# Four groups of seven block products in the second down projection, with the weight sums made in HBM

## Chip, cores and metric

One core of a Trainium2 chip runs the whole program, once per launch, in float32. The metric is the device time of one execution in microseconds (us).

## What is computed

Two transformer blocks over 256 tokens of width 1024. The first holds two mixers (forgetting attention and a gated delta rule) and a gated feed-forward part; the second holds neighbourhood attention, a pooling mixer and a gated feed-forward part of hidden width 2816. The change sits in the last product of the second block:

```python
h2 = rms_norm(x, norm2_g[l])
x = x + (jax.nn.silu(h2 @ w_gate[l]) * (h2 @ w_up[l])) @ w_down[l]
```

`w_down` is 2816 x 1024, so this last product takes 256 x 2816 by 2816 x 1024.

## The kernel before

TensorE multiplies float32 as sums of two parts: each weight panel is copied to `panel_hi` by ScalarE (ACT), VectorE (DVE) makes the residual `panel_lo`, and each 128-row tile of a product takes three matmuls (hi by hi, lo by hi, hi by lo). All weight products of both blocks stand in one list, `HALVES`, of 258 **steps**. A plain step uses half a panel: 12 matmuls of 512 columns in the last product. Four buffers each of `panel_hi` and `panel_lo` go round (`whi`, `wlo`): the copy of step n waits until the product of step n - 4 is done (`s_half`). The panels come by SP's DMA queue into three 1 MB buffers `panel_raw`, refilled when the residual of their last step is made (`s_lo`); at the start three more, `panel_raw_early`, are filled ahead. Every engine walks the same list in program order, so an instruction that waits holds all that stands behind it on its engine.

The last product uses seven products in place of eight on part of its rows (Winograd's form of Strassen's scheme). A **group** is 512 rows of `w_down`. Split in even and odd 128-row tiles and in two halves of 512 columns, it gives the blocks b11, b12, b21, b22 (512 KB each); the 256 tokens are two halves. Then

- t1 = b11 + b12, t3 = b12 + b22, t2 = t1 + b22, t4 = t2 + b21 are sums of weight blocks (signs lie in the activations),
- GpSimd (POOL) makes four sums of activations for each pair of row tiles (`act2_sums`), split in hi and lo by ACT and DVE,
- seven **block steps** (b11, b21, b22, t3, t1, t2, t4) of 6 matmuls each go into seven PSUM banks, and DVE combines the banks at the end (`block_sums`).

`GROUP_ORDER` says in which order block steps stand, and where plain steps (`None`) stand between them. Before there are two groups, with every block step but one followed by a plain step; the other 1792 of the 2816 rows are plain. The four blocks of a group are loaded during the product before (`up2`), and the sums are made by DVE in place (`add_block`), each right behind the residual of a block.

Ahead of all this stands the first block's input projection. Its first panels and the small tensors load from the start of the span. POOL's work in that part: one power at the start, one for the key norms (step 17), a mask for each attention head (`mask_key_bias`, which waits for a load of that head), and gate arithmetic.

Of the kernel before, what the change touches and what calls it, by code (L numbers as in the profile page):

```python
# [23 lines left out]
P = 128  # L24
# [46 lines left out]
for _name, _n in (("ident", P), ("upper", P), ("ones", 4), ("causal", P), ("decay_mask", P),  # L71
# [142 lines left out]
TAIL_AT = {n: j for n, (s, j) in TAP_AT.items() if s == 1}  # L214
BLOCKS_FROM = [END["up2", 1, 4], END["up2", 1, 6]]
UP2_AT = {}
# [21 lines left out]

def build(nc, a, out, scratch_a, scratch_x, scratch_c):
    ctx = ExitStack()  # L240
    with ctx:
# [5 lines left out]
        def at(name, shape, unit, dt=F32, skip=0):  # L247
            return nc.alloc_sbuf_tensor_at(name, shape, dt, offset=BASE + int(unit * UNIT) + skip)[:]
# [61 lines left out]
        sq2 = at("sq2", [P, TT, 2, PW], 23.5)  # L310
        block_at = [{"b11": 22, "b12": 22.5, "b21": 23, "b22": 23.5}, {"b11": 0, "b12": 0.5, "b21": 16.5, "b22": 21.5}]
        block_raw = [{b: at(f"block_{b}_{i}", [P, HALF * PW], block_at[i][b]) for b in BLOCKS} for i in range(2)]
        act_sums = [at(f"act_sums{i}", [P, 4, P], 21, skip=2048 * i) for i in range(2)]
        act_sums_hi = at("act_sums_hi", [P, 2 * GROUPS, 4, P], 18, F32R)
        act_sums_lo = at("act_sums_lo", [P, 2 * GROUPS, 4, P], 19.5, F32R)
        sum_u, sum_v, minus_w, p5_less_v = [at(f"block_sum{i}", [P, WIDE], 1, skip=2048 * i) for i in range(4)]
        mixh, mixl = at("mix_hi", [P, KD, T], 11, F32R), at("mix_lo", [P, KD, T], 12, F32R)
# [182 lines left out]
        s_g_low, s_g_row, s_half_rsq = sem("ffn2_low_copied"), sem("ffn2_gate_scaled"), sem("half_row_rms")  # L500
        s_block = [[sem(f"block_row{r}_landed{i}") for r in range(2)] for i in range(2)]
        s_block_add = sem("blocks_added")
        s_sums, s_sums_hi, s_sums_lo = sem("act_sums"), sem("act_sums_hi"), sem("act_sums_lo")
# [90 lines left out]
        def block_rows(g, b):  # L594
            r, c = int(b[1]) - 1, int(b[2]) - 1
            w = weights["w_down_2"][g * HALF * P:(g + 1) * HALF * P, wide(c)]
            return w.rearrange("(k r p) c -> r p k c", r=2, p=P)[r]

# [3 lines left out]

        KEPT_IN = {b: b for b in BLOCKS} | {"t1": "b11", "t3": "b12", "t2": "b22", "t4": "b21"}
        OTHER = {"t1": "b12", "t3": "b22", "t2": "b11", "t4": "b22"}
        ADDS = list(ADDED_BEHIND.values())

        def block_landed(g, b):
            return s_block[g][int(b[1]) - 1], 32

        def block_added(g, b):  # L610
            return s_block_add, len(ADDS) * g + ADDS.index(b) + 1

        def block_ready(g, b):
            return block_landed(g, b) if b in BLOCKS else block_added(g, b)

# [618 lines left out]
        def scalar_program(e):  # L1234
# [3 lines left out]
            def split(n):  # L1238
                if n > STEPS:
                    return  # L1240
                i, k0, kt = HALVES[n - 1]
                if i is None:
                    g, b = k0, kt
                    e.wait_ge(*block_ready(g, b))
                    e.wait_ge(s_half, n - 4)
                    copy(whi[(n - 1) % 4], block_raw[g][KEPT_IN[b]]).then_inc(s_hi, 1)
# [483 lines left out]
        def vector_program(e):  # L1730
            def add_block(g, b, n):
                t_ = ADDED_BEHIND[b]
                to = block_raw[g][KEPT_IN[t_]]
                e.wait_ge(*block_landed(g, OTHER[t_]))
                e.wait_ge(s_lo, n)
                if ADDS.index(t_):
                    e.wait_ge(s_block_add, len(ADDS) * g + ADDS.index(t_))
                e.tensor_tensor(to, to, block_raw[g][OTHER[t_]], ALU.add).then_inc(s_block_add, 1)  # L1738
# [750 lines left out]
        def pool_program(e):  # L2489
# [36 lines left out]
            def act2_sums(j):  # L2526
# [14 lines left out]
            for n in range(1, STEPS + 1):  # L2541
                if n == 27:
                    e.wait_ge(s_consts, 16)
                    mask_key_bias(0)
# [44 lines left out]
        def sync_program(e):  # L2589
            def fetch(i):  # L2590
# [8 lines left out]
                for s in range(parts):  # L2599
                    e.dma_start(dst[:, :, s * n:(s + 1) * n], w_rows(weights[w], k0, kt, c0 + s * apart, n)) \  # L2600
                        .then_inc(raw_landed(i)[0], 16)

            x_rows = a["x"][0].rearrange("(t p) d -> p t d", p=P)
            for c in range(2):
# [10 lines left out]
            for n in range(1, STEPS + 1):  # L2615
                for i in range(9, len(PLAN)):
                    if LAST_HALF[BEFORE[i]] + 1 == n + 3:
                        fetch(i)
                for g in range(GROUPS):
                    for at_, b in zip(range(0, 8, 2), ("b11", "b12", "b21", "b22")):  # L2620
                        if n == BLOCKS_FROM[g] + at_:
                            e.wait_ge(*emptied(("out2", 1, 1)))
                            e.dma_start(block_view(block_raw[g][b]), block_rows(g, b)).then_inc(block_landed(g, b)[0], 16)
                if n == 3:
# [139 lines left out]
```

## Time and profile before

| | |
|---|---|
| Median of 3 runs | 802.75 us (802.33 to 803.99) |
| The profiled execution | 802.98 us, span 801.5 us |
| TensorE busy | 795.6 us (99% of the span), 5164 matmuls recorded |
| DVE, ACT, POOL busy | 625.1, 457.2, 90.7 us |
| DMA | 144.09 MB, 180 GB/s over the span |
| Granted TensorE clock | full speed throughout |

A busy share says how long some instruction ran on an engine. Matmuls overlap each other: their durations add up to more than the time they take, so the time of a run of matmuls is read from its start and end.

### The profile page before, as it was taken

Reading aid. Unit: us, or ns where it says so; the run is one execution under the profiler, and the core shown is the slowest. Engines: PE = TensorE matmul, PEld = TensorE weight load, DVE = VectorE, ACT = ScalarE, POOL = GpSimd, SP = SyncE. Lnnn points to the kernel's source line nnn. Section 1 sums busy time; section 2 is a strip of 40 time slices with the busy share of each in tenths; the row PEclk is TensorE's granted clock in tenths of the full one; section 3 lists DMA queues with packets and bytes.
Section 4 is the critical chain, followed back from the end, with each engine's and each line's share of the span. In section 5 each row is a group of like instructions: output and inputs, shape, how many; then the busy total and the mean of one; then the engine's idle time right before and its main releaser. Section 6 shows DMA issues by size and latency. Waiting matters only on the chain. (4 is left out here: it accounts for less than half of the span.)

```text
span 801.5 us, 13178 instructions
## 1 busy us (share of the span) xinstructions
PE 795.6 (99%) x5164; PEld 696.8 (87%) x5164; DVE 625.1 (78%) x1035; ACT 457.2 (57%) x738; POOL 90.7 (11%) x77
## 2 busy tenths in 40 slices
PE   8999999999999999999999999999999999999998
PEld 6888888999898888899999998887778888888886
DVE  6888989785555766679999997486866898787977
ACT  6667677554535544456656563466665566555552
POOL 0001000010011302101101110011100333011100
PEclk9999999999999999999999999999999999999999
DMA  9654564557432555475687656464424666884331
GB/s 317 187 166 157 176 229 145 151 146 228 123 118 88 172 173 199 167 237 180 193 251 244 224 186 209 165 203 160 156 79 147 198 207 214 288 282 161 107 103 54
DMA packets 118125, 144.09 MB, mean 180 GB/s; under 512 B 11552, under 2 KB 86704, under 8 KB 117808
## 3 DMA queue, kind: packets, MB, share of 16 engines
q1 hardware_dynamic: 115616, 141.22, 54.7%
q10 hardware_dynamic: 2448, 2.03, 1.0%
q8 instruction: 41, 0.67, 0.3%
q14 instruction: 20, 0.16, 0.1%
HBM read 141.78 MB, written 1.46 MB: 179 GB/s over the span
## 5 line engine op out<-in xcount | busy, mean ns | idle before, releaser
L1754 DVE TENSOR_TENSOR panel_lo<-panel_raw,panel_hi 128x1024 fp32r<-128x1024 f32 x237 | 300.8, 1272 | 106.8 <-ACT panel_hi L1236 105.1
L652 PE MATMUL bank<-x_halves,panel_hi 128*128 128x256 f32 (+1 forms) x1536 | 367.0, 322 | 0.7 <-DVE x_halves L2222 0.7
L1236 ACT ACTIVATE panel_hi<-panel_raw 128x1024 fp32r<-128x1024 f32 (+1 forms) x239 | 252.2, 1057 | 152.9 <-PE bank L652 150.8
L652 PE MATMUL bank<-x_halves,panel_lo 128*128 128x256 f32 x1024 | 288.3, 282 | 0.0
L652 PEld LDWEIGHTS bank<-x_halves,panel_hi 128*128 128x128 f32 x1536 | 255.8, 190 | 23.3 <-issue 0.9
L652 PEld LDWEIGHTS bank<-x_halves,panel_lo 128*128 128x128 f32 x1024 | 195.0, 190 | 0.2
L652 PE MATMUL bank<-panel_hi,x_halves 128*128 128x512 f32 x384 | 122.1, 399 | 0.0
L652 PEld LDWEIGHTS bank<-panel_hi,x_halves 128*128 128x128 f32 x384 | 70.0, 188 | 14.4 <-DVE panel_lo L1754 0.6
L652 PE MATMUL bank<-panel_lo,x_halves 128*128 128x512 f32 x192 | 75.1, 391 | 0.0
L652 PE MATMUL bank<-panel_hi,act_hi 128*128 128x512 f32 x156 | 60.9, 390 | 0.2 <-DVE panel_lo L1754 0.2
L652 PE MATMUL bank<-panel_hi,act_lo 128*128 128x512 f32 x156 | 60.7, 389 | 0.0
L652 PE MATMUL bank<-panel_lo,act_hi 128*128 128x512 f32 x156 | 60.7, 389 | 0.0
L652 PEld LDWEIGHTS bank<-panel_lo,x_halves 128*128 128x128 f32 x192 | 36.0, 188 | 8.0
L2491 POOL TENSOR_TENSOR stats<-stats 128x2 f32<-128x2 f32 (+1 forms) x9 | 17.1, 1900 | 185.1 <-DVE stats L1768 104.0
L652 PEld LDWEIGHTS bank<-panel_hi,act_hi 128*128 128x128 f32 x156 | 29.3, 188 | 6.6 <-DVE panel_lo L1754 0.6
L652 PEld LDWEIGHTS bank<-panel_lo,act_hi 128*128 128x128 f32 x156 | 29.3, 188 | 6.1
L652 PEld LDWEIGHTS bank<-panel_hi,act_lo 128*128 128x128 f32 x156 | 29.3, 188 | 5.9
L1790 DVE SCALAR_TENSOR_TENSOR conv_acc<-conv_tmp,params,conv_acc 128x255 f32<-128x255 f32 (+2 forms) x72 | 30.5, 484 | 1.4 <-ACT conv_acc L1236 1.4
L2517 POOL TENSOR_TENSOR ff_tanh<-ff_tanh,ff_val 128x512 f32<-128x512 f32 x11 | 17.2, 1564 | 112.4 <-DVE ff_tanh L2115 112.4
L2496 POOL TENSOR_TENSOR key_bias<-key_bias,constants 128x128 f32<-128x128 f32 x16 | 8.9, 577 | 176.6 <-DMA key_bias<-gate_sums 176.6
L2524 POOL TENSOR_TENSOR f_tanh<-f_tanh,ff_val 128x512 f32<-128x512 f32 x11 | 15.2, 1385 | 94.0 <-DVE f_tanh L2191 94.0
L1748 DVE TENSOR_TENSOR panel_lo<-block_b,panel_hi 128x1024 fp32r<-128x1024 f32 x14 | 18.2, 1301 | 5.2 <-ACT panel_hi L1236 4.8
(312 smaller groups left out, 1017.1 us busy)
## 6 DMA issues: line engine op xcount, KB each, us to landing
panel_raw<-in_w_in SPq DMA_DIRECT2D x35, 1024.0 KB, 5.3
panel_raw<-in_w_up SPq DMA_DIRECT2D x30, 1024.0 KB, 5.4
panel_raw<-in_w_down SPq DMA_DIRECT2D x16, 1024.0 KB, 5.0
panel_raw<-in_w_gate SPq DMA_DIRECT2D x10, 1024.0 KB, 5.4
panel_raw<-in_w_out SPq DMA_DIRECT2D x8, 1024.0 KB, 5.0
panel_raw<-in_w_in SPq DMA_DIRECT2D x11, 512.0 KB, 4.7
panel_raw<-in_w_branch_fox SPq DMA_DIRECT2D x4, 1024.0 KB, 5.0
panel_raw<-in_w_branch_gdn SPq DMA_DIRECT2D x4, 1024.0 KB, 5.0
```

The costliest lines, as they stand in the source:

```text
L652: return e.matmul(o, l, r, start=start, stop=stop, skip_group_check=True)
L1236: return e.activation(o, i_, ACT.Copy, scale=scale)
L1748: e.tensor_tensor(wlo[w], block_raw[g][KEPT_IN[b]], whi[w].bitcast(F32), ALU.subtract) \
L1754: e.tensor_tensor(lo, raw_view(i, k0, kt), hi.bitcast(F32), ALU.subtract).then_inc(s_lo, 1)
L1790: e.scalar_tensor_tensor(acc[:, f, back:], tmp[:, f, 0:T - back], gconv(p, f, back), acc[:, f, back:], ALU.mult, ALU.add).then_inc(s_taps, 1)
L2491: return e.tensor_tensor(cols, cols, minus_half.broadcast_to([P, n]), ALU.pow)
L2496: i_ = e.tensor_tensor(key_bias[:, s], key_bias[:, s], C("causal"), ALU.add)
L2517: e.tensor_tensor(th, th, ff_acc[j % 2][1], ALU.mult).then_inc(s_f_mul, 1)
L2524: e.tensor_tensor(th, th, ff_acc[j % 2][1], ALU.mult).then_inc(s_g_mul, 1)
```

## The change

Groups go from two to four (2048 rows), and plain steps from 14 to 6. The weight sums are no longer made by DVE in SBUF: POOL issues 32 transfers from HBM to HBM, 16 copies and 16 that accumulate into their destination, into a new HBM tensor `weight_sums` of 16 blocks of 512 KB. SP then loads the seven blocks of each group (three of `w_down`, four sums) into a ring of ten 512 KB buffers, two sharing a semaphore. The diff (cut):

```diff
-GROUPS = 2
-DOWN2_ORDER = [(8, 0), (8, 1), (12, 0), (12, 1), (16, 0), (20, 0), (16, 1), (20, 1)]
+GROUPS = 4
+DOWN2_ORDER = [(16, 0), (16, 1), (20, 0), (20, 1)]
-GROUP_ORDER = [("b11", None, "b21", None, "b22", None, "t3", None, "t1", None, "t2", None, "t4", None),
-               ("b11", None, "b21", None, "b22", None, "t3", None, "t1", "t2", None, "t4", None, None)]
-ADDED_BEHIND = {"b11": "t1", "b21": "t3", "b22": "t2", "t3": "t4"}
+GROUP_ORDER = [(None, "b11", "b21", "b22", "t3", "t1", "t2", "t4"),
+               (None, "b11", "b21", "b22", "t3", "t1", "t2", "t4"),
+               ("b11", "b21", "b22", "t3", "t1", "t2", "t4"),
+               ("b11", "b21", "b22", "t3", "t1", "t2", "t4", None, None, None, None)]
+WEIGHT_SUMS = ("t1", "t3", "t2", "t4")
+SUM_ROUNDS = (2, 5, 7, 8)
+SUMS_FROM, SUMS_EVERY = 11, 5
+SUMS_AT = {SUMS_FROM + SUMS_EVERY * i: divmod(i, len(SUM_ROUNDS)) for i in range(GROUPS * len(SUM_ROUNDS))}
...
-                    e.tensor_tensor(wlo[w], block_raw[g][KEPT_IN[b]], whi[w].bitcast(F32), ALU.subtract) \
-                        .then_inc(s_lo, 1)
-                    if b in ADDED_BEHIND:
-                        add_block(g, b, n)
+                    e.tensor_tensor(wlo[w], block_buffer(g, b), whi[w].bitcast(F32), ALU.subtract).then_inc(s_lo, 1)
...
+            def copied(g, t_, b):
+                e.dma_start(sum_rows(g, t_), block_rows(g, b)).then_inc(s_weight_sums, 16)
+            def added(g, t_, what):
+                e.dma_start(sum_rows(g, t_), what, accum_op=ALU.add, max_dma_last_dim=4 * WIDE).then_inc(s_weight_sums, 16)
+            def weight_sums(g, stage):
+                done = SUM_ROUNDS[-1] * g + (SUM_ROUNDS[stage - 1] if stage else 0)
+                if done:
+                    e.wait_ge(s_weight_sums, 16 * done)
+                if stage == 0:
+                    copied(g, "t1", "b11")
+                    copied(g, "t3", "b12")
+                if stage == 1:
+                    added(g, "t1", block_rows(g, "b12"))
+                    added(g, "t3", block_rows(g, "b22"))
+                    copied(g, "t2", "b22")
+                if stage == 2:
+                    added(g, "t2", sum_rows(g, "t1"))
+                    copied(g, "t4", "b21")
+                if stage == 3:
+                    added(g, "t4", sum_rows(g, "t2"))
...
+                for q, (g, b) in enumerate(BLOCK_SEQ):
+                    if q < 6 and n == BLOCKS_FROM + 2 * q:
+                        e.wait_ge(*emptied(("out2", 1, 1)))
+                        fetch_block(q, g, b)
+                    if 6 <= q < len(block_raw) and n == END["up2", 1, KF // 2 - 1] + 1:
+                        e.wait_ge(*product(("up2", 1, KF // 2 - 1)))
+                        fetch_block(q, g, b)
+                    if q >= len(block_raw) and n + 3 == BLOCK_AT[BLOCK_SEQ[q - len(block_raw)]]:
+                        e.wait_ge(s_lo, n + 3)
+                        fetch_block(q, g, b)
```

So a group's sums are made in four **stages** (0 to 3), placed at POOL's steps 11, 16, 21 and so on up to 86. Each stage waits for all transfers of the stage before.

POOL's program begins so before (`stats` holds the small vectors of the norms, and the four rows of `key_bias` shown as x12 are masks of attention heads):

```order
L2491 TENSOR_TENSOR stats<-stats 128x2
L2491 TENSOR_TENSOR stats<-stats 128x16
L2496 TENSOR_TENSOR key_bias<-key_bias,constants 128x128 x12
L2503 TENSOR_SCALAR gate_f<-gate_f 128x512 x2
```

and so after, with stages 0 and 1 of the first group ahead of the key norms and all four of the second between the masks of heads 0 and 1:

```order
L2490 TENSOR_TENSOR stats<-stats 128x2
L2537 DMA weight_sums<-in_w_down 256x1x512 x2
L2540 DMA weight_sums<-in_w_down 256x1x512 x2
L2537 DMA weight_sums<-in_w_down 256x1x512
L2490 TENSOR_TENSOR stats<-stats 128x16
L2540 DMA weight_sums<-weight_sums 256x512
L2537 DMA weight_sums<-in_w_down 256x1x512
L2540 DMA weight_sums<-weight_sums 256x512
L2495 TENSOR_TENSOR key_bias<-key_bias,constants 128x128 x2
```

The power at the start is now followed by five transfers that wait for no other engine's work, only for each other.

ACT's copies near the end stood so before, around the copy of one product's bank (`block_sum`), which waits for that product and for a DVE addition:

```order
L1236 ACTIVATE panel_hi_58<-block_b_1_141 128x1024
L1236 ACTIVATE panel_hi_59<-panel_raw_50 128x1024
L1236 ACTIVATE block_sum_147<-bank 128x512
L1236 ACTIVATE panel_hi_56<-block_b_1_142 128x1024
L1236 ACTIVATE panel_hi_57<-panel_raw_50 128x1024
```

and after it stands in the fourth group, between blocks:

```order
L1247 ACTIVATE panel_hi_58<-block_137 128x1024
L1247 ACTIVATE panel_hi_59<-block_138 128x1024
L1247 ACTIVATE panel_hi_56<-block_139 128x1024
L1247 ACTIVATE block_sum_149<-bank 128x512
L1247 ACTIVATE panel_hi_57<-block_140 128x1024
```

The steps on both sides of it are now block steps of 6 matmuls, where plain steps of 12 stood between blocks.

## Rows read from the trace of the kernel before

**Rows 1.** The page's first part: engine, busy us and share, instructions.

```profile
PE 795.6 (99%) x5164; PEld 696.8 (87%) x5164; DVE 625.1 (78%) x1035; ACT 457.2 (57%) x738; POOL 90.7 (11%) x77
```

**Rows 2.** The chain that ended last: start us, us, what.

```profile
754.89 43.83 PE bank L652 x192
...
798.74 0.48 DVE h L2083
```

**Rows 3.** The timeline at the last product's first matmul: start us, us, what.

```profile
740.88 0.39 PE L652 MATMUL bank<-panel_hi,act_hi 128*128 128x512 f32 x1
```

**Rows 4.** Instruction groups by shape, 742 to 801.5 us: count, busy us, mean ns, idle before.

```profile
L1754 DVE TENSOR_TENSOR panel_lo<-panel_raw,panel_hi 128x1024 fp32r<-128x1024 f32 x13 | 15.9, 1222 | 3.0 <-ACT panel_hi L1236 2.7
...
L1236 ACT ACTIVATE panel_hi<-block_b 128x1024 fp32r<-128x1024 f32 x12 | 12.7, 1060 | 5.1 <-PE bank L652 5.1
...
L1738 DVE TENSOR_TENSOR block_b<-block_b,block_b 128x1024 f32<-128x1024 f32 x7 | 8.6, 1226 | 1.0 <-issue 0.5
...
L2050 DVE SCALAR_TENSOR_TENSOR h<-bank,stats,h 128x512 f32<-128x512 f32 x1 | 0.7, 746 | 0.0
```

**Rows 5.** ACT's timeline in the last product: start us, us, what, idle before.

```profile
750.73 0.64 ACT L1236 ACTIVATE act_hi<-f_tanh 128x512 fp32r<-128x512 f32 x1 [3.04 <-POOL f_tanh L2524]
...
773.25 0.60 ACT L1236 ACTIVATE block_sum<-bank 128x512 f32<-128x512 f32 x1 [1.95 <-DVE h L2050]
773.75 1.05 ACT L1236 ACTIVATE panel_hi<-block_b 128x1024 fp32r<-128x1024 f32 x1
```

**Rows 6.** The page's DMA issues: count, KB each, median us to landing.

```profile
panel_raw<-in_w_in SPq DMA_DIRECT2D x35, 1024.0 KB, 5.3
...
block_b<-in_w_down SPq DMA_DIRECT2D x8, 512.0 KB, 7.2
...
panel_raw<-in_w_down SPq DMA_DIRECT2D x4, 512.0 KB, 3.5
```

**Rows 7.** Stretches: us, busy us of PE to POOL, clock, DMA share, GB/s.

```profile
8.00:12.00 4.00, 2.95 (x19) 1.94 (x19) 3.62 (x9) 3.29 (x7) 0.07 (x1) 1.00 1.10 348
16.00:20.00 4.00, 4.00 (x36) 4.00 (x35) 4.00 (x11) 2.99 (x4) 0.00 (x0) 1.00 1.07 363
24.00:28.00 4.00, 4.00 (x24) 3.47 (x23) 3.19 (x6) 3.16 (x6) 0.00 (x0) 1.00 1.07 371
...
32.00:36.00 4.00, 4.00 (x22) 3.35 (x21) 4.00 (x10) 2.62 (x3) 0.00 (x0) 1.00 0.25 71
...
200.00:250.00 50.00, 50.00 (x465) 43.93 (x462) 26.04 (x55) 22.95 (x48) 4.89 (x8) 1.00 0.34 103
```

**Rows 8.** The tile panel_raw_early: its loads (first and last start), and time to landing.

```profile
L2600 SPq DMA_DIRECT2D panel_raw_early<-in_w_in x3: 1420/2025/2832, 5.2 to 10.2; - x3
...
DMA to landing us min/median/max: 10.7/11.3/11.5
```

**Rows 9.** ACT's timeline, copies of the second and third early panel.

```profile
23.69 1.06 ACT L1236 ACTIVATE panel_hi<-panel_raw_early 128x1024 fp32r<-128x1024 f32 x1 [0.60 <-PE bank L652]
...
26.52 1.06 ACT L1236 ACTIVATE panel_hi<-panel_raw_early 128x1024 fp32r<-128x1024 f32 x1 [0.55 <-PE bank L652]
```

**Rows 10.** POOL's timeline: the first power, and masks of heads 0, 1, 4 and 6.

```profile
7.35 0.72 POOL L2491 TENSOR_TENSOR stats<-stats 128x2 f32<-128x2 f32 x1 [6.54 <-DVE stats L1768]
...
108.76 1.06 POOL L2496 TENSOR_TENSOR key_bias<-key_bias,constants 128x128 f32<-128x128 f32 x2 [38.70 <-DMA key_bias<-gate_sums]
171.37 0.89 POOL L2496 TENSOR_TENSOR key_bias<-key_bias,constants 128x128 f32<-128x128 f32 x2 [61.54 <-DMA key_bias<-gate_sums]
...
206.71 0.88 POOL L2496 TENSOR_TENSOR key_bias<-key_bias,constants 128x128 f32<-128x128 f32 x2 [9.56 <-DMA key_bias<-gate_sums]
...
237.07 0.88 POOL L2496 TENSOR_TENSOR key_bias<-key_bias,constants 128x128 f32<-128x128 f32 x2 [12.19 <-DMA key_bias<-gate_sums]
```

**Rows 11.** Waits over the span: us in total, times, longest us.

```profile
DVE fox_p L1998 <- POOL key_bias L2496: 2.8, 3, 1.6
...
ACT panel_hi L1236 <- DMA panel_raw<-in_w_in: 2.0, 3, 0.8
```

More of the change, by code:

```diff
@@ L83 @@
 DOWN_ORDER = [(k, c) for k in range(0, KF - 6, HALF) for c in range(2)] + [(k, c) for c in range(2) for k in (16, 20)]
-GROUPS = 2
-DOWN2_ORDER = [(8, 0), (8, 1), (12, 0), (12, 1), (16, 0), (20, 0), (16, 1), (20, 1)]
+GROUPS = 4
+DOWN2_ORDER = [(16, 0), (16, 1), (20, 0), (20, 1)]
 BLOCKS = ("b11", "b12", "b21", "b22")
-GROUP_ORDER = [("b11", None, "b21", None, "b22", None, "t3", None, "t1", None, "t2", None, "t4", None),
-               ("b11", None, "b21", None, "b22", None, "t3", None, "t1", "t2", None, "t4", None, None)]
-ADDED_BEHIND = {"b11": "t1", "b21": "t3", "b22": "t2", "t3": "t4"}
+GROUP_ORDER = [(None, "b11", "b21", "b22", "t3", "t1", "t2", "t4"),
+               (None, "b11", "b21", "b22", "t3", "t1", "t2", "t4"),
+               ("b11", "b21", "b22", "t3", "t1", "t2", "t4"),
+               ("b11", "b21", "b22", "t3", "t1", "t2", "t4", None, None, None, None)]
+BLOCK_SEQ = [(g, b) for g, order in enumerate(GROUP_ORDER) for b in order if b]
+WEIGHT_SUMS = ("t1", "t3", "t2", "t4")
+SUM_ROUNDS = (2, 5, 7, 8)
+SUMS_FROM, SUMS_EVERY = 11, 5
 BLOCK_BANK = {"b11": ("p1",), "b21": ("down2", 0, 0), "b22": ("down2", 1, 0), "t4": ("down2", 0, 1), "t1": ("p5",),
@@ L214 @@
 TAIL_AT = {n: j for n, (s, j) in TAP_AT.items() if s == 1}
-BLOCKS_FROM = [END["up2", 1, 4], END["up2", 1, 6]]
+BLOCKS_FROM = END["up2", 1, 4]
+SUMS_AT = {SUMS_FROM + SUMS_EVERY * i: divmod(i, len(SUM_ROUNDS)) for i in range(GROUPS * len(SUM_ROUNDS))}
 UP2_AT = {}
@@ L236, with build @@
 GA_EXP, GA_BETA, GA_COEF, GA_KDEC, GA_MINUS_EGC = 1, 2, 3, 4, 6
-def build(nc, a, out, scratch_a, scratch_x, scratch_c):
+def build(nc, a, out, scratch_a, scratch_x, scratch_c, scratch_w):
     ctx = ExitStack()
@@ L310, in build @@
         sq2 = at("sq2", [P, TT, 2, PW], 23.5)
-        block_at = [{"b11": 22, "b12": 22.5, "b21": 23, "b22": 23.5}, {"b11": 0, "b12": 0.5, "b21": 16.5, "b22": 21.5}]
-        block_raw = [{b: at(f"block_{b}_{i}", [P, HALF * PW], block_at[i][b]) for b in BLOCKS} for i in range(2)]
-        act_sums = [at(f"act_sums{i}", [P, 4, P], 21, skip=2048 * i) for i in range(2)]
+        block_at = (22, 22.5, 23, 23.5, 0, 0.5, 1, 1.5, 2, 2.5)
+        block_raw = [at(f"block{i}", [P, HALF * PW], unit) for i, unit in enumerate(block_at)]
+        act_sums = [at(f"act_sums{i}", [P, 4, P], 16.5, skip=2048 * i) for i in range(2)]
         act_sums_hi = at("act_sums_hi", [P, 2 * GROUPS, 4, P], 18, F32R)
-        act_sums_lo = at("act_sums_lo", [P, 2 * GROUPS, 4, P], 19.5, F32R)
-        sum_u, sum_v, minus_w, p5_less_v = [at(f"block_sum{i}", [P, WIDE], 1, skip=2048 * i) for i in range(4)]
+        act_sums_lo = at("act_sums_lo", [P, 2 * GROUPS, 4, P], 20, F32R)
+        sum_u, sum_v, minus_w, p5_less_v = [at(f"block_sum{i}", [P, WIDE], 10, skip=2048 * i) for i in range(4)]
         mixh, mixl = at("mix_hi", [P, KD, T], 11, F32R), at("mix_lo", [P, KD, T], 12, F32R)
@@ L500, in build @@
         s_g_low, s_g_row, s_half_rsq = sem("ffn2_low_copied"), sem("ffn2_gate_scaled"), sem("half_row_rms")
-        s_block = [[sem(f"block_row{r}_landed{i}") for r in range(2)] for i in range(2)]
-        s_block_add = sem("blocks_added")
+        s_block = [sem(f"blocks_landed{i}") for i in range(len(block_at) // 2)]
+        s_weight_sums = sem("weight_sums_written")
         s_sums, s_sums_hi, s_sums_lo = sem("act_sums"), sem("act_sums_hi"), sem("act_sums_lo")
@@ L596, in block_rows, with sum_rows, block_source, block_buffer @@
             w = weights["w_down_2"][g * HALF * P:(g + 1) * HALF * P, wide(c)]
-            return w.rearrange("(k r p) c -> r p k c", r=2, p=P)[r]
+            return w.rearrange("(k r p) c -> r k p c", r=2, p=P)[r]
+        def sum_rows(g, t_):
+            return scratch_w[g, WEIGHT_SUMS.index(t_)].rearrange("(k p) c -> k p c", p=P)
+        def block_source(g, b):
+            return (block_rows(g, b) if b in BLOCKS else sum_rows(g, b)).rearrange("k p c -> p k c")
         def block_view(t_):
             return t_.rearrange("p (k c) -> p k c", c=WIDE)
-        KEPT_IN = {b: b for b in BLOCKS} | {"t1": "b11", "t3": "b12", "t2": "b22", "t4": "b21"}
-        OTHER = {"t1": "b12", "t3": "b22", "t2": "b11", "t4": "b22"}
-        ADDS = list(ADDED_BEHIND.values())
+        def block_buffer(g, b):
+            return block_raw[BLOCK_SEQ.index((g, b)) % len(block_raw)]
+        def block_sem(q):
+            return s_block[q // 2 % len(s_block)]
         def block_landed(g, b):
[L608 to L614, printed above, removed]
+            q = BLOCK_SEQ.index((g, b))
+            return block_sem(q), 16 * sum(block_sem(i) is block_sem(q) for i in range(min(q | 1, len(BLOCK_SEQ) - 1) + 1))
         def rows_of(sums, h0, n):
@@ L1243, in split @@
                     g, b = k0, kt
-                    e.wait_ge(*block_ready(g, b))
+                    e.wait_ge(*block_landed(g, b))
                     e.wait_ge(s_half, n - 4)
-                    copy(whi[(n - 1) % 4], block_raw[g][KEPT_IN[b]]).then_inc(s_hi, 1)
+                    copy(whi[(n - 1) % 4], block_buffer(g, b)).then_inc(s_hi, 1)
                     return
@@ L1730, in vector_program @@
         def vector_program(e):
[L1731 to L1738, printed above, removed]
             def split(n):
@@ L2541, in pool_program @@
             for n in range(1, STEPS + 1):
+                if n in SUMS_AT:
+                    weight_sums(*SUMS_AT[n])
                 if n == 27:
@@ L2601, in fetch, with fetch_block @@
                         .then_inc(raw_landed(i)[0], 16)
+            def fetch_block(q, g, b):
+                if b not in BLOCKS:
+                    e.wait_ge(s_weight_sums, 16 * SUM_ROUNDS[-1] * GROUPS)
+                e.dma_start(block_view(block_raw[q % len(block_raw)]), block_source(g, b)).then_inc(block_sem(q), 16)
             x_rows = a["x"][0].rearrange("(t p) d -> p t d", p=P)
@@ L2618, in sync_program @@
                         fetch(i)
[L2619 to L2623, printed above, removed]
+                for q, (g, b) in enumerate(BLOCK_SEQ):
[8 more added lines that the diff above has]
+                        fetch_block(q, g, b)
                 if n == 3:
@@ L2760 @@
     sc = nc.dram_tensor("gate_sums", (2, HEADS, T), F32).ap()
-    build(nc, args, out, sa, sx, sc)
+    sw = nc.dram_tensor("weight_sums", (GROUPS, len(WEIGHT_SUMS), PW, WIDE), F32).ap()
+    build(nc, args, out, sa, sx, sc, sw)
     r = run_bass_kernel_spmd(nc, [arrays], core_ids=[0])
```

## The prediction

> **What bounds the kernel now.** I read the page's busy shares first: TensorE is busy for 795.6 of 801.5 us [rows 1]. A busy share of matmuls proves little, so I looked for waits. The chain that ended last goes back over 43.83 us of unbroken matmuls, and behind them stand only DVE's last additions [rows 2]. Over the whole span ACT's copies waited for a panel's load 2.0 us in three cases, so loads are hidden almost everywhere [rows 11]. TensorE is the bound from some 10 us to the end. What the change saves on TensorE is saved in full, and every wait that it puts before TensorE costs in full: there is no slack downstream to take it up.
>
> **TensorE's saving.** Before, the last product has 14 plain steps of 12 matmuls and 14 block steps of 6: 252. After, 6 plain and 28 block steps: 240. The unbroken stretch gives 43.83 us for 192 matmuls, 228.3 ns each [rows 2] (the 390 ns or so that one lasts by itself is no price, as they overlap). Twelve fewer: **-2.74 us**. The whole product ran from 740.88 to 798.72 us, 57.84 us [rows 2, 3]; after, that would be 55.1.
>
> **DVE and ACT in the last product.** DVE loses eight additions of 1.23 us, ACT and DVE gain six steps' copies (1.06 us) and residuals (1.22 us) [rows 4]. That is not the point; the pace is. A block step is 6 x 228.3 = 1.37 us of TensorE, and now up to fourteen and more follow each other without a plain step between. The copy of step n starts when product n - 4 is done; copy and residual take 2.28 us, and three block steps give 4.11. So 1.8 us is spare at each step, and DVE's 1.22 us per step fits in 1.37. It holds, but nothing else may stand in the way for long. Two things do:
>
> - Behind the last gate products ACT waits for POOL's product (3.04 us idle before `act_hi` [rows 5]), and the copies of the next blocks stand behind that. Before, this ended in a short wait of TensorE just ahead of 754.89 us (the unbroken stretch starts there). Block steps reach the place sooner, but DVE's additions there are gone; I take it as unchanged, 0.
> - The copy of the first product's bank (`block_sum`). Put 0 where TensorE ends the last b11. DVE is then at the residual of the step three ahead: copy from -1.37 to -0.3, residual to 0.9. Its addition of 0.75 us [rows 4] ends at 1.65; ACT copies the bank, and its next block copy starts 0.50 us later [rows 5], at 2.15 or somewhat over, and ends at 3.2; the residual ends at 4.45. TensorE wants it at 4.11. With signals between engines I take **+0.5 us**; without them it is 0.3, with a second such wait 1.0.
>
> **Loads in the last product.** Six blocks are loaded before it, as eight were. Left are 22 blocks and a panel of 512 KB, 12.0 MB. The highest rates that the trace holds over some microseconds are 348 to 371 GB/s [rows 7]; at 360, 12.0 MB takes 33.4 us, and the last landing is some 3.5 us behind its issue [rows 6]: 37. The last block step ends at 55.1 less four plain steps (11.0) = 44.1, so its copy must start by 40.4. That leaves 3 us. One block takes 1.46 us to load and 1.37 to use, so the ring of ten falls back by 0.09 us a block, 2 us over 22. I take 0. At 300 GB/s the 12.0 MB take 40.0 us and the end comes 3 us late.
>
> **The 32 transfers of the sums.** The trace holds no transfer from HBM to HBM, none that accumulates and none issued by POOL. I bound them by passes of 512 KB at 360 GB/s, 1.46 us each: below, one pass a transfer (47 us of all DMA engines together); above, every read and write counts, two passes for a copy and three for an accumulation (117 us). They are spread over some 310 us, in which the DMA share is at places as low as 0.34 [rows 7]. What counts is where they meet a tight load or hold POOL.
>
> - *The start.* POOL's first power ends at 8.1 us [rows 10], and stage 0 follows at once: into the stretch where the DMA engines are full, until 28 us [rows 7]. Panels in flight are held back by what the sums put between their packets. The first early panel lands at 5.2 + 10.7 = 15.9 us [rows 8]; TensorE ends step 4 at 23.7 [rows 9], so its copy must start by 23.7 - 2.28 = 21.4: 5.5 us spare, against 2.9 to 5.8 us for stage 0 (2 to 4 passes). The third lands at 10.2 + 11.5 = 21.7 at most; step 5 ends at 26.5 [rows 9], three steps of 2.83 later step 9 begins, at 35.0, and the copy must start by 32.7: 11.0 us spare, against stages 0 and 1 together, 7.3 to 17.4 us (5 to 12 passes). So the cost is 0 to 6.4 us. I take **+0.3**: of all rows a plain load, one pass, is nearest to these, and DMA falls to a share of 0.25 by 32 us [rows 7], so what is late then is caught up.
> - *POOL's queue.* A stage waits for the one before it, and masks stand behind it. The second group's four stages lie between the masks of heads 0 and 1, where POOL idled 61.5 us [rows 10]; stages 0 to 2 take at most 17 passes (25 us) and three landings of 7.2 us [rows 6], 46. In the third group stage 1 is issued behind the mask of head 4, at 207.6 us, and stage 2, which waits for it, stands ahead of that of head 6, at 237.07 [rows 10]: 29.5 us, against 8 passes and a landing, 19. DVE waits for these masks as it is, by up to 1.6 us [rows 11], so a late one goes straight to TensorE. I take 0.
> - *Accumulating beside panels elsewhere.* Loads of 1 MB land 5.3 us after issue [rows 6] and were hardly ever waited for. 0, with up to 2 us if two stages meet a tight panel.
>
> **Sum.** 802.98 (the profiled execution; 1.5 us lie outside its span) - 2.74 + 0.5 + 0.3 = 801.0; that execution lies 0.2 above the median of the runs, so **800.8 us**.
>
> **Rivals.**
>
> *A. The early panels are late.* For it: the full DMA engines until 28 us, and that nothing holds stage 0 back. Against it: 5.5 and 11 us of slack. Above 1 of the 6.4 us, the time is 801.8 to 807. It decides from the point where stages 0 and 1 cost the third early panel over 11 us, so some 7 to 8 passes.
>
> *B. The transfers run on few of the DMA engines.* A copy's source is 2 rows of tiles x 128 x 512, its destination 256 x 512. If the split over engines goes by the outer size 2, two engines carry 256 KB each. A full engine moves 360 / 16 = 22.5 GB/s, so that is 11.7 us for one pass, 35 for three. Then panels that share those two engines wait for them. Stage 0 on the first early panel: 6.4 us of its bytes remain at 9.5 us, and as many of the copy go between them, 6.4 us at one pass and 12.8 at two, against 5.5: 0.9 to 7.3 us late. And stage 1 with three passes takes 35 + 7.2 = 42 us against 29.5 at head 6: its mask is 12.7 us late. Light form: about 802. Heavy form: 7.3 + 12.7 on top, near 820. Nothing in the trace speaks for or against it, since all DMAs there have 128, 64, 16 or 8 rows outermost.
>
> The Trainium skill has a rule of just this form ("DMA: Bandwidth & Descriptors", section "Why a DMA increments its semaphore by 16 and not by 1"): the engine count is the largest one up to 16 that divides the slowest size of both patterns, which would be 2 here, with an exception for some direct copies of GpSimd that get all 16. No run here shows it. By that rule the time is that of rival B, by its exception that of the sum.
>
> *C. The blocks come late in the last product.* 28 block steps want 0.524 MB in 1.37 us, 383 GB/s, above anything that the trace shows for long. For it: the eight block loads before landed in 7.2 us, though issued behind a panel. Against it: ten buffers. At 300 GB/s: 803.8; at 270 (12.0 MB in 44.4 us), 808. It decides below some 330 GB/s.
>
> *D. The product runs without any wait*, those of before gone with DVE's additions: 802.75 - 2.74 - 0.4 = 799.6.
>
> **How the numbers follow.** A difference under 0.2% (1.6 us: under 801.15 is faster, over 804.35 slower) can hardly be told from none here. The forecast has 0.50, and lies near that line: 0.36 of it faster, 0.14 not told from before. A 0.16 (0.07 same, 0.09 slower). B 0.18 (light 0.08 same, heavy 0.10 slower). C 0.10 (0.01 same, 0.09 slower). D 0.06, faster. So faster 0.42, same 0.30, slower 0.28. The range 799.0 to 810 leaves out the heavy half of B and the far end of the gains; the forecast's own is 799.8 to 802.
>
> **What would show it.** Right: some 240 matmuls in about 55.5 us from the first one on `act_hi` to the end; a wait of TensorE of 0.5 us behind the last b11; ACT's copies in the last product released by products, not by DMA. In the first 40 us TensorE as busy as before, the early panels landing 3 to 7 us later. POOL's masks at the same distance from their loads. Wrong: ACT's waits for `panel_raw` or blocks far over 2 us in total; masks that wait for `weight_sums`; a DMA share in the last product at its ceiling with ACT waiting for blocks. Most likely to break the forecast are the prices of the accumulations, of which no row tells.

## The result and the profile after

The changed kernel takes 930.9 us (median of 6 runs, 927.47 to 938.86) against 802.44 us: a ratio of 1.1604, 95% interval 1.1576 to 1.1633. The forecast was 800.8 us, the range to 810. So the loss is 128 us, and it lies ahead of the last product, as the stretches of the profile after show (the stretch, then its length and the busy us and count of PE, PEld, DVE, ACT and POOL; then granted clock, DMA share, GB/s):

```profile
150.00:200.00 50.00, 35.88 (x255) 34.69 (x254) 23.71 (x56) 15.90 (x21) 4.91 (x3) 0.86 0.52 131
200.00:250.00 50.00, 25.73 (x336) 25.11 (x337) 14.33 (x31) 10.26 (x20) 7.76 (x9) 0.73 0.56 134
...
396.00:405.00 9.00, 0.00 (x0) 0.00 (x0) 0.00 (x0) 0.00 (x0) 0.00 (x0) 0.50 0.14 33
400.00:450.00 50.00, 12.35 (x50) 10.47 (x51) 6.25 (x7) 5.29 (x6) 7.51 (x6) 0.58 0.35 86
```

TensorE, busy without a gap from 200 to 250 us before [rows 7], is busy for half of that stretch and for a quarter of 400 to 450. From 396 to 405 us no engine computes at all. Where TensorE stands still the granted clock falls to 0.50, the lower level (1.2 GHz); so its busy time over the span rises to 810.0 us, with 12 matmuls fewer.

Whom does it wait for? TensorE's waits after (us in total, times, longest):

```profile
PE bank L801 <- POOL gate_g L2587: 48.5, 2, 45.6
PE bank L663 <- DVE stats L1997: 47.9, 4, 26.5
PE bank L663 <- DVE panel_lo L1753: 9.5, 3, 6.7
...
DVE fox_p L1997 <- POOL key_bias L2495: 65.1, 5, 29.6
```

`gate_g` is written by POOL's gate sums, and L1997 is the line of DVE that waits for POOL's masks (the last row: 65.1 us in five cases; 2.8 us before [rows 11]). Four fifths of TensorE's waits of 118 us go back to POOL, and POOL's own timeline says what it does (start, us, what, and idle time before with its releaser):

```profile
8.05 1.32 POOL L2537 DMA_DIRECT2D weight_sums<-in_w_down  x1
...
31.37 3.85 POOL L2540 DMA_DIRECT2D weight_sums<-in_w_down  x2 [20.90 <-DMA weight_sums<-in_w_down]
...
222.37 1.17 POOL L2495 TENSOR_TENSOR key_bias<-key_bias,constants 128x128 f32<-128x128 f32 x2
...
261.36 1.90 POOL L2540 DMA_DIRECT2D weight_sums<-in_w_down  x1
292.47 1.90 POOL L2540 DMA_DIRECT2D weight_sums<-in_w_down  x1 [29.20 <-issue]
293.55 1.93 POOL L2537 DMA_DIRECT2D weight_sums<-in_w_down  x1
294.65 1.71 POOL L2495 TENSOR_TENSOR key_bias<-key_bias,constants 128x128 f32<-128x128 f32 x2
...
451.51 2.78 POOL L2587 TENSOR_TENSOR gate_g<-gate_g,gate_f 128x512 f32<-128x512 f32 x2
```

Two things hold it. Between stages it waits for its own transfers: 164.9 us in eleven cases, such as the 20.90 us before 31.37. And five times it stands idle ahead of a *further* transfer of the same stage, named "issue" because no semaphore explains it (29.20 us ahead of 292.47, while the addition issued at 261.36 is under way): 115.8 us. In the waits after (us in total, times, longest; one more, of 1.7 us, is for another kind of transfer):

```profile
POOL weight_sums L2540 <- DMA weight_sums<-in_w_down: 163.2, 10, 24.9
...
POOL weight_sums L2540 <- issue: 62.7, 2, 33.5
...
POOL weight_sums L2537 <- issue: 53.1, 3, 30.9
```

The mask of head 1, at 171.37 us before [rows 10], comes at 222.37; the last gate sum, in POOL's timeline before at

```profile
319.68 3.54 POOL L2563 TENSOR_TENSOR gate_g<-gate_g,gate_f 128x512 f32<-128x512 f32 x2 [8.27 <-DVE gate_g L2022]
```

comes at 451.51, 131.8 us later, right behind the last transfer, and TensorE waits 45.6 us for a gate sum. That is the whole loss to within half a microsecond: the span grew by 129.4 us, and the last product won 2.0.

Why do the transfers take so long? The page's issues (count, KB, median us to landing):

```profile
panel_raw<-in_w_in SPq DMA_DIRECT2D x35, 1024.0 KB, 11.4
...
weight_sums<-in_w_down POOLq DMA_DIRECT2D x24, 512.0 KB, 17.0
...
weight_sums<-weight_sums POOLq DMA_DIRECT2D x8, 512.0 KB, 6.9
...
panel_raw_early<-in_w_in SPq DMA_DIRECT2D x3, 1024.0 KB, 21.0
```

A transfer between two contiguous places (an addition too) lands in 6.9 us, one from `w_down` in 17.0 at the median and an addition from there in up to 35.3. In 396 to 405 us above one addition is alone with the end of a panel's load, and the DMA share is 0.14, at 33 GB/s: two of sixteen engines are 0.125. The queues in that stretch (q0 is POOL's, q1 SP's):

```profile
q0 software_dynamic: 73, 0.15, 8.9%
q1 hardware_dynamic: 72, 0.14, 4.8%
```

The two queues moved almost equal numbers of packets, 73 and 72, with little more than two engines busy: as it seems, the panel's last packets take turns with the addition's on the same two engines. A panel of `w_in` now lands in 11.4 us, 5.3 before [rows 6], and the early ones in 21.0, 11.3 before [rows 8]. Per transfer the engine time is small: in 264 to 290 us q0 shows 13.8% of 16 engines, 57 engine-microseconds for an addition. Over two engines that is 29 us at most, over sixteen 3.6 (estimates).

The last product went as worked out: from its first matmul at 872.31 to the end of the last at 928.12, 55.8 us (forecast 55.6; 57.84 before [rows 2, 3]). The wait of 0.5 us behind the last b11 is there too (the first row is the first matmul; then the chain of the profile after, TensorE idle from 912.33):

```profile
872.31 0.39 PE L663 MATMUL bank<-panel_hi,act_hi 128*128 128x512 f32 x1
...
883.47 23.43 PE bank L663 x102
...
909.22 0.76 DVE h L2049
...
910.00 0.02 ACT block_sum L1247
...
912.86 15.27 PE bank L663 x66
```

### The profile page after: what moved, and what is told of

It reads as the page before. It is cut to its first block, busy times and chain, and to the rows that moved or that the text cites. A ratio compares the mean times of both kernels' runs of the same rounds, so it can differ in the third digit from the quotient of the medians.

```text
span 930.9 us, 13244 instructions
## 1 busy us (share of the span) xinstructions
PE 810.0 (87%) x5152; PEld 707.9 (76%) x5152; DVE 628.7 (68%) x1037; ACT 464.6 (50%) x748; POOL 141.9 (15%) x121
## 4 chain that ended last, share of the span: by engine, by line
PE 53%; DMA 23%; issue 14%; DVE 5%; POOL 3%; ACT 1%; SPq 1%; ACTq 0%; DVEq 0%; POOLq 0%
PE bank L663 51%; DMA weight_sums<-in_w_down 15%; DMA panel_raw<-in_w_in 3%; DMA panel_raw_early<-in_w_in 2%; DVE panel_lo L1753 2%; DVE conv_acc L1789 1%; POOL weight_sums L2540 1%; DMA key_bias<-gate_sums 1%; DMA weight_sums<-weight_sums 1%; DVE panel_lo L1750 1%; ACT panel_hi L1247 1%; POOL gate_g L2587 1%; PE bank L779 1%; DMA gate_sums<-minus_c_rows 1%; PE bank L1101 0%
## 5 line engine op out<-in xcount | busy, mean ns | idle before, releaser
L663 PE MATMUL bank<-x_halves,panel_hi 128*128 128x256 f32 (+1 forms) x1536 | 374.2, 326 | 13.7 <-DVE panel_lo L1753 9.5
L1753 DVE TENSOR_TENSOR panel_lo<-panel_raw,panel_hi 128x1024 fp32r<-128x1024 f32 x229 | 291.8, 1277 | 104.6 <-ACT panel_hi L1247 102.0
L1247 ACT ACTIVATE panel_hi<-panel_raw 128x1024 fp32r<-128x1024 f32 (+1 forms) x231 | 243.5, 1055 | 171.8 <-PE bank L663 138.4
L663 PEld LDWEIGHTS bank<-x_halves,panel_hi 128*128 128x128 f32 x1536 | 262.0, 195 | 37.5 <-DVE panel_lo L1753 10.5
L663 PE MATMUL bank<-panel_hi,act_hi 128*128 128x512 f32 x136 | 53.1, 391 | 0.1
L663 PE MATMUL bank<-panel_lo,act_hi 128*128 128x512 f32 x136 | 52.9, 389 | 0.0
L663 PE MATMUL bank<-panel_hi,act_lo 128*128 128x512 f32 x136 | 52.9, 389 | 0.0
L663 PE MATMUL bank<-fox_pT,vf 128*128 128x128 f32 x48 | 9.5, 348 | 47.9 <-DVE stats L1997 47.9
L1997 DVE CUSTOM_DVE_ANT_0 fox_p<-bank,key_bias 128x128 f32<-128x128 f32 (+1 forms) x16 | 5.1, 354 | 67.3 <-POOL key_bias L2495 65.1
L663 PEld LDWEIGHTS bank<-fox_pT,vf 128*128 128x128 f32 x48 | 7.9, 241 | 49.1 <-DVE stats L1997 48.9
L1750 DVE TENSOR_TENSOR panel_lo<-block,panel_hi 128x1024 fp32r<-128x1024 f32 x28 | 34.9, 1261 | 7.1 <-ACT panel_hi L1247 5.2
## 6 DMA issues: line engine op xcount, KB each, us to landing
panel_raw<-in_w_in SPq DMA_DIRECT2D x35, 1024.0 KB, 11.4
```

What stands on the lines that cost most here:

```text
L663: return e.matmul(o, l, r, start=start, stop=stop, skip_group_check=True)
L1247: return e.activation(o, i_, ACT.Copy, scale=scale)
L1750: e.tensor_tensor(wlo[w], block_buffer(g, b), whi[w].bitcast(F32), ALU.subtract).then_inc(s_lo, 1)
L1753: e.tensor_tensor(lo, raw_view(i, k0, kt), hi.bitcast(F32), ALU.subtract).then_inc(s_lo, 1)
L1997: i_ = e.tensor_tensor_reduce(pb[:, s], bank[:, s], key_bias[:, s], -1.0, -3 * NEG, ALU.add, ALU.min, nm[:, m:m + 1])
```

## Experiments

**Sixteen engines, and no transfers at all.** First theory (E): the outer sizes, 256 and 2, put a transfer on two engines. `spread` turns both sides so that 128 rows stand outermost:

```diff
-                e.dma_start(sum_rows(g, t_), block_rows(g, b)).then_inc(s_weight_sums, 16)
+                e.dma_start(sum_rows(g, t_).rearrange("k p c -> p k c"), block_rows(g, b).rearrange("k p c -> p k c")).then_inc(s_weight_sums, 16)
```

and the same in `added`.

> Both sides of all 32 transfers are written with 128 rows outermost (128 x 2 x 512 instead of 256 or 2 x 128 outermost); same bytes, same places, same waits. Theory E (few engines: the outer sizes 256 and 2 put a transfer on two DMA engines): a transfer from w_down takes about a sixteenth of its 30 or 60 engine-microseconds, 2 to 4 us, plus a few us of landing, so copies land in 4 to 7 us instead of 17 and additions in 6 to 9 instead of 30; masks and gate sums are back at their old times; 800 to 806 us. Rival H (it is the reading and writing of HBM within an accumulation that is slow, on however many engines): additions from w_down stay above 20 us, the time above 860 us. Rival Q (POOL's own issuing is slow): issue lengths and idle times named issue stay, the time above 880 us.

Measured: 806.77 us, ratio 1.0052 (1.0035 to 1.0069). Of 128 us, 124 are gone by the order of sizes alone. Its issues:

```profile
weight_sums<-in_w_down POOLq DMA_DIRECT2D x24, 512.0 KB, 7.2
...
panel_raw_early<-in_w_in SPq DMA_DIRECT2D x3, 1024.0 KB, 13.8
```

No idle time named issue is left, and DVE waits for masks 2.4 us in all. E holds, H and Q fall. The turned form also leaves fewer packets, so one may ask whether it is their number that cost. First the change, then `spread` (packets and sizes of all queues; POOL's packets, MB and share of 16 engines):

```profile
DMA packets 156782, 167.39 MB, mean 180 GB/s; under 512 B 40992, under 2 KB 116144, under 8 KB 156464
...
q0 software_dynamic: 35328, 17.01, 9.5%
...
DMA packets 128110, 167.17 MB, mean 207 GB/s; under 512 B 12320, under 2 KB 87472, under 8 KB 127792
...
q0 software_dynamic: 6656, 16.78, 8.8%
```

The 28,672 packets that are gone are all under 512 B (8 bytes each in the trace). The 6,144 packets that carry POOL's data are the same in both, and by size in the two traces they take 1,154 us of engine time in the change and 1,134 in `spread`. The work is the same; it lies on more engines.

What remains lies 0.8 us above E's range. TensorE waits 4.6 us for DVE's `kT`, and the chain before it starts with the third early panel (start, us, what):

```profile
9.91 21.41 DMA panel_raw_early<-in_w_in
...
41.32 0.61 DVE kT L1803
```

`no_sums` leaves the transfers out and prices the rest of the change:

```diff
-                if n in SUMS_AT:
-                    weight_sums(*SUMS_AT[n])
...
-            return (block_rows(g, b) if b in BLOCKS else sum_rows(g, b)).rearrange("k p c -> p k c")
+            return block_rows(g, {"t1": "b11", "t3": "b12", "t2": "b22", "t4": "b21"}.get(b, b)).rearrange("k p c -> p k c")
...
```

and SP's wait for the sums goes too.

> The 32 transfers are left out, and the 16 blocks of sums are loaded from the places of plain blocks in w_down instead, so the last product computes with unsummed blocks; everything else as in the change. This prices all of the change but the transfers. Theory: only the last product differs from before, 55.8 us against 57.84, so 800.4 us (799.8 to 801.2), a ratio of 0.9975. Rival: some of the 128 us comes from elsewhere in the change (buffers moved, blocks issued between panels), then above 802.5 us.

Measured: 800.22 us, ratio 0.9973 (0.9961 to 0.9985). Without the transfers the change gains 2.3 us, 2.0 of it in the last product; all of the loss belongs to the transfers.

**Four engines.** `four` makes each transfer two of 256 KB with 4 outermost:

```diff
-                e.dma_start(sum_rows(g, t_), block_rows(g, b)).then_inc(s_weight_sums, 16)
+                for k in range(2):
+                    to, what = (t.rearrange("k (p a) c -> k a p c", a=4)[k] for t in (sum_rows(g, t_), block_rows(g, b)))
+                    e.dma_start(to, what).then_inc(s_weight_sums, 16)
```

> Each transfer is two of 256 KB, each with an outer size of 4 on both sides (rows taken in the order 4 x 32). Theory E: four engines for each half, so an addition of 256 KB has half of the 60 engine-microseconds over four engines, 7.5 us, and a copy 3.8 us, plus landing: 9 to 12 and 6 to 8 us; the time is 803 to 825 us, far nearer to spread than to 930.9. Rival H: additions remain near 30 us or above. If the count of engines follows something other than the outer size (128 rows in all, say), it equals spread.

Measured: 815.34 us in one run, idle times named issue 32.4 us, and landings of

```profile
weight_sums<-in_w_down POOLq DMA_DIRECT2D x48, 256.0 KB, 9.4
```

With 2, 4 and 128 outermost the time is 931, 815 and 807 us, so it follows the outer size and not the rows in all. (`four` also halves the transfers, so that a stage has twice as many, which may lie on different engines.) That is the Trainium skill's rule ("DMA: Bandwidth & Descriptors", section "Why a DMA increments its semaphore by 16 and not by 1"): the engine count is the largest number up to 16 that divides the slowest size of both sides. The DMA share of 0.14, the 6.9 us of the contiguous transfers (256 outermost on both sides) and these three times agree with it. So do the packets of 8 bytes. The change has 28,672 of them and `four` 18,432. That is 14 and 12 times the data packets that one of two or of four engines would carry, 2,048 and 1,536, as if each idle engine got a small packet in place of each of these (estimate, from the packet counts); `spread` has none. The rule's exception for some of GpSimd's direct copies did not apply here.

**POOL's queue or the loads?** `dve_masks` leaves the transfers as changed and moves masks, affine maps and gate sums to VectorE:

```diff
-                e.wait_ge(s_kb, hh + 1)
+                e.wait_ge(s_kb_in, 32 * (hh + 1))
+                for s in (slice(0, P), slice(2 * P, 3 * P)):
+                    i_ = e.tensor_tensor(key_bias[:, s], key_bias[:, s], C("causal"), ALU.add)
+                i_.then_inc(s_kb, 1)
+                e.wait_ge(s_kb, hh + 1)
```

and likewise in `branch`, with POOL's calls taken out.

> As changed, two-engine transfers and all, but the causal masks, the affine maps of the gates and the gate sums are done by VectorE instead of POOL, so that nothing that TensorE waits for by way of masks and gate sums stands behind a transfer in POOL's queue. Theory P (the time is lost in POOL's queue): the 96 us of TensorE's waits for masks (47.9) and gate sums (48.5) go, and with them most of the time at the lower clock; 815 to 840 us. Rival L (the loads of panels that share the two engines are what is slow, and the masks only hide it): 870 to 920 us, with the waits now at panel_lo behind panel_raw.

Measured: 891.21 us in one run, in L's range, but not by L's mechanism: `panel_lo` accounts for 12.4 us of TensorE's waits, and the longest is

```profile
PE bank L811 <- POOL stats L2501: 30.2, 1, 30.2
```

the next instruction that stands behind the transfers in POOL's program, the power behind the output projection:

```profile
439.23 0.90 POOL L2551 DMA_DIRECT2D weight_sums<-weight_sums  x1 [14.58 <-DMA weight_sums<-in_w_down]
439.84 1.04 POOL L2501 TENSOR_TENSOR stats<-stats 128x2 f32<-128x2 f32 x1
```

Before it stood at

```profile
349.04 1.62 POOL L2491 TENSOR_TENSOR stats<-stats 128x2 f32<-128x2 f32 x1 [25.82 <-DVE stats L1768]
```

It is 90.8 us late, and the span is 88.4 us longer (90.4 with the 2.0 won at the end). Of its 440 us up to there POOL waits 347 for its own transfers or at their issue, so I read what TensorE loses earlier, to loads, as lying in the shadow of POOL's chain. So I had left out that POOL's queue has a next customer; P's mechanism holds, its price does not.

**Place or form?** `two_89_5` moves the two-engine transfers as they are to a part without masks:

```diff
-SUMS_FROM, SUMS_EVERY = 11, 5
+SUMS_FROM, SUMS_EVERY = 89, 5
```

> The change's own two-engine transfers, at the steps of spread_89_5 (89 to 164). In the change POOL waited 280.7 us for its own transfers or at their issue, and some 30 us went into issuing: 310 us for 16 stages, 19 a stage, where five steps take 14. Theory F (the form of the transfers is what costs, wherever they lie): POOL falls behind by 5 to 7 us a stage, its gate products and powers with it, and TensorE waits for them: 860 to 910 us, with idle times named issue over 60 us. Rival G (the early place, in front of masks and small transfers, is what costs): 801 to 830 us.

Measured: 978.35 us in one run, beyond F's 910. POOL now holds the first feed-forward, and then `norm_gained`, which stands behind the last stage but one (waits in us in total, times, longest; POOL's timeline, before and in `two_89_5`):

```profile
ACT act_hi L1247 <- POOL ff_tanh L2516: 137.5, 10, 37.0
...
DVE norm_junk L1759 <- POOL norm_gained L2508: 53.2, 1, 53.2
...
523.32 2.84 POOL L2509 TENSOR_TENSOR norm_gained<-h,gain_final 128x1024 f32<-128x1024 f32 x1 [43.06 <-DVE h L2032]
...
700.20 1.43 POOL L2537 DMA_DIRECT2D weight_sums<-in_w_down  x1
701.29 2.70 POOL L2508 TENSOR_TENSOR norm_gained<-h,gain_final 128x1024 f32<-128x1024 f32 x1
```

It is 178.0 us late, and the span is 175.5 us longer. The loss is again the lateness of POOL. The panels that land late have moved with the transfers: `w_in` takes 5.3 us again, `w_up` 10.4 instead of 5.4. Form, not place.

**What holds POOL at the issue?** `free_copies` issues 32 two-engine copies, each to a place of its own, without any wait; `free_half` the same with half of the rows. The last product takes unsummed blocks in both.

```diff
-                done = SUM_ROUNDS[-1] * g + (SUM_ROUNDS[stage - 1] if stage else 0)
-                if done:
-                    e.wait_ge(s_weight_sums, 16 * done)
...
+                for slot in range(SUM_ROUNDS[stage - 1] if stage else 0, SUM_ROUNDS[stage]):
+                    copied(g, slot, BLOCKS[slot % 4])
```

> All 32 transfers are plain copies of blocks in the change's own two-engine form, each to a place of its own, so no stage waits for the one before it; the sums are not made and the last product takes unsummed blocks. Nothing in the program holds POOL any more. Theory I (POOL is held at the issue itself, while an earlier transfer is still on its two engines): idle times named issue of 15 us and more ahead of further copies, over 60 us in total, masks late behind them, 820 us or more. Rival S (it was the waits between the stages that held POOL): no such idle times, masks on time, 801 to 808 us, what is left being panels that share engines.

Measured: 829.17 us in one run, idle times named issue 59.3 us in four cases. POOL's timeline, the first of them:

```profile
77.31 2.17 POOL L2538 DMA_DIRECT2D weight_sums<-in_w_down  x2
96.86 1.06 POOL L2538 DMA_DIRECT2D weight_sums<-in_w_down  x1 [17.39 <-issue]
```

The holds come at the 8th, 15th, 22nd and 29th copy. So I is right that POOL is held with no wait in the program. But no mask was late by it (1.8 us of waiting for masks in all). Of the 27 us over the kernel before, TensorE's longest waits show 16.4: 6.6 us for the small transfer of `XT` of the inversion, 5.3 for `panel_lo`, 4.5 for a convolution. I read them as loads that share engines with the copies; the rest is not accounted for.

> As free_copies with the first half of each block's rows alone: 32 two-engine copies of 256 KB, no waits between them. In free_copies POOL was held at the 8th, 15th, 22nd and 29th copy. Theory R (what fills up at the issue is room that goes by the bytes or rows of a transfer): held at about the 15th or 16th and the 29th or 30th alone. Theory N (it goes by the number of transfers): held at the 8th, 15th, 22nd and 29th again. By either the loads are disturbed half as much: 808 to 818 us.

Measured: 805.02 us in one run, a smaller disturbance than either theory said; held twice, at the 16th copy (12.35 us) and the 31st:

```profile
130.07 0.81 POOL L2538 DMA_DIRECT2D weight_sums<-in_w_down  x1 [12.35 <-issue]
...
294.84 0.80 POOL L2538 DMA_DIRECT2D weight_sums<-in_w_down  x1 [12.86 <-issue]
```

So seven copies of 512 KB pass between two holds, and fifteen of 256 KB: theory R. Their queues count 33280 and 16896 packets, 1040 and 528 a copy; 7 x 1040 = 7280 and 15 x 528 = 7920 fit, 8 x 1040 = 8320 and 16 x 528 = 8448 do not. So there is room for about 8,000 packets (estimate, from these counts), and the copy that finds none waits until those under way have ended. It is not the bytes: `spread` moves the same bytes in 6656 packets and was never held. Nor is it only the packets under way: five of the first seven copies in `free_copies` were issued by 14 us and no copy took over 30.0 us to land, so these five had ended long before the hold that began at 79 us. The count seems to go on until it is full and to start afresh there. In the change itself, with additions among the copies, the holds do not fall where this count alone puts them: that is open. They do go by the order of the transfers and not by the time, since they stand at the 7th, 10th, 13th, 20th and 28th transfer in the change, in `dve_masks` and in `two_89_5`.

**The early panels, and a version that gains.** `spread` with the stages elsewhere: steps 18, 23, ... (behind the power of the key norms), 18, 22, ..., then 89, 94, ... and 100, 104, .... The edit is the line of numbers shown for `two_89_5`.

> As spread, with the first stage at step 18 instead of 11, so that POOL comes to it only behind the power of the key norms (66 us) and no transfer meets the early panels; stages 5 steps apart as in the change. Theory A (what spread still lacks of 800.2 is only the early panels that come late, 6.5 us): 800.0 to 801.0 us, a ratio of 0.997 to 0.9985, DVE's wait for kT gone, the early panels landing after 11.3 us again. Rival B2 (the transfers cost about the same wherever they lie, in panels that come late or masks that wait): 803 to 807 us.

> As spread_18_5 with the stages 4 steps apart, so the last lies at step 78 and ahead of the gate sums. Theory A: as spread_18_5 within 0.5 us. Rival B2: 1 to 3 us more than spread_18_5, since the stages lie closer to the masks and a stage that waits for the one before it holds POOL up to 9 us.

Measured: 802.06 and 802.11 us, ratios 0.9995 (0.9985 to 1.0005) and 0.9997 (0.9984 to 1.001). Between A and B2: the early panels land after 11.4 us again and DVE's wait for `kT` is gone, 4.7 us won, but 1.9 us are still missing. Some of it lies from 150 to 200 us. In `spread_18_4` (a profile of a run at the median) TensorE is idle there for 1.3 us, in `spread_18_5` (a profile of a run of 804.76 us, 2.7 above the median) for 1.2 us, for other reasons:

```profile
PE bank L1050 <- DVE fox_p L2008: 1.3, 1, 1.3
...
PE bank L663 <- DMA X<-blocks_inverted: 1.2, 1, 1.2
```

Their runs differ by up to 5 us, so this is no full account.

> As spread, with the stages at steps 89, 94, ... 164, all behind the inversion's small transfers and the masks, over the first feed-forward, in which POOL has only gate products with 10 us between them. Theory A2 (the 1.9 us that spread_18_5 and spread_18_4 lack of 800.2 are meetings with the small transfers and loads of 150 to 200 us): 800.0 to 800.9 us, ratio 0.997 to 0.9985, faster than before. Rival B2 (16 MB more through the DMA engines cost 2 us wherever they lie): 801.5 to 803 us.

> As spread_89_5 at steps 100 to 160, closer together and clear of the power behind the output projection (step 97). Theory A2: within 0.4 us of spread_89_5. Rival B2: 801.5 us or more.

Measured: 800.83 and 800.69 us, ratios 0.9974 (0.9964 to 0.9985) and 0.9975 (0.9964 to 0.9985): A2, and both faster than the kernel before, by a quarter of a per cent. Over the first feed-forward the 16 MB cost at most 0.6 us against `no_sums`; a panel of `w_up` lands in 6.0 us there, and POOL waits up to 10 us for its transfers. ACT waits 7.7 us in all for POOL's products there; TensorE shows one wait of 0.4 us for a residual. The page's busy shares, over a span of 799.8 us:

```profile
PE 792.1 (99%) x5152; PEld 693.8 (87%) x5152; DVE 627.2 (78%) x1037; ACT 463.7 (58%) x748; POOL 140.1 (18%) x121
```

## Why the prediction was wrong, point by point

- **TensorE's saving, DVE and ACT in the last product, loads there:** right. 55.8 us for 55.1 + 0.5, the wait at `block_sum` in its place, the 22 blocks and the panel on time; `no_sums` 800.22 us. Rivals C and D fall.
- **The price of the transfers:** right as a sum, wrong in its shape; this is the first step that failed. In bounds of 47 to 117 us of all DMA engines, the trace has 9.5% of 16 engines over 930.9 us, 88 us. The prediction took passes at 360 GB/s, the rate of all engines, because "of all rows a plain load, one pass, is nearest": but a plain load has 128 rows outermost, and these have 256 against 2. The time to land is what stages and panels wait for: 17.0 us at the median on two engines, 7.2 with 128 outermost.
- **Rival B** named this, with 11.7 us for one pass and 35 for three (measured: copies land in 17.4 us at the median, an addition keeps its two engines for up to 29), and the chance was set to 0.18 because no row spoke for or against it. The sizes stood in the diff, but no row before says what they do. The form was right; its time of 820 was not, for the reason that follows.
- **POOL's queue, "I take 0":** the second failed step, and the larger one. Even rival B counted one late mask, 12.7 us, and ended near 820. Two things were missing. The stages follow each other on POOL, so their lateness adds up over four groups instead of being lost at one mask: what counts is how late the instruction behind the transfers is that others still wait for (131.8 us in the change, 90.8 in `dve_masks`, 178.0 in `two_89_5`, each within 1 us of the loss and the 2 us won at the end). And POOL is also held at the issue, 115.8 us of the change, which no row before shows. No run tells how much of the lateness is these holds and how much the slow landings: `spread` takes both away.
- **The start, +0.3 (rival A at 0.16):** hidden in the change behind the rest, but wrong once the transfers are spread: moving the stages behind the early panels, from `spread` to `spread_18_5`, is worth 4.7 us, inside rival A's 0 to 6.4. The slack was counted to the wrong place. In `spread` the third early panel lands at 31.3 us instead of 21.7 at most, 9.6 us late and within the 11.0 us up to TensorE's own step; but DVE's convolutions stand behind its residual, and TensorE waits for `kT`, which they feed.
- **Loads elsewhere, "hardly ever waited for", 0 to 2 us:** also wrong for two-engine transfers: in the change ACT's copies wait 28.2 us in six cases for panels of `w_in`, 2.0 before [rows 11], and TensorE waits 9.5 us for residuals.

## What to carry to other kernels

Before a transfer is priced, look at the outermost sizes of both its sides as the instruction carries them: merged rows on one side and a size of 2 on the other put it on two engines here, and a turned pattern with the same bytes took 124 of 128 us back. On an engine that issues transfers and waits for them, add up the landings of the whole chain and ask how late the first instruction behind it comes; moving another engine's work out of the way only finds the next one. And a transfer that nobody waits for still has to be put where no load is tight: the same 16 MB cost 6.5, 1.9 and at most 0.6 us at three places.

## What was not expected of the hardware

- POOL stands still when it issues a further transfer, with no semaphore to wait for, after every 7,280 packets of copies in `free_copies` and 7,920 in `free_half`, also where part of them had long landed; the next one had to wait for those under way. In the change such a hold lasted up to 33.5 us.
- The count of packets depends on the form: 1040 for a two-engine copy of 512 KB, of which 896 are of 8 bytes, and 208 on average for the transfers of `spread`, with none of 8 bytes.
- Two transfers of this form in flight at once seem to lie on different pairs of engines: from 412 to 432 us of the change a copy and an addition run together at a DMA share of 0.24, 3.8 engines of sixteen, where one alone has 0.13 to 0.14.
